# Hybrid trunk on one core: experts' tokens permuted once per layer, VectorE adds the result from PSUM

## What is computed

```python
g_prob = softmax(h @ wg + bg);  g_p, g_idx = top_k(g_prob, 1)
e_p, e_idx = top_k(softmax(e_logits of that group), 2)
gate = g_p * e_p / sum(e_p)
for e in range(16):
    a = silu(h @ w_gate[e]) * (h @ w_up[e])
    y = y + combine[:, e] * (a @ w_down[e])
return x + y
```

## Time and profile before

| | us |
|---|---|
| median of three runs | 1746.99 |
| the profiled execution | 1747.63 |
| its span, first to last instruction | 1745.8 |
| TensorE busy in the span | 1637.6 (94%) |
| VectorE busy | 1432.2 (82%) |
| ScalarE busy | 1087.4 (62%) |
| GpSimd busy | 91.3 (5%) |

### The profile page before, as it was taken

One profiled execution on the slowest core, in us unless ns is written; L12 is line 12 of the kernel. 1 busy time (PEld: TensorE's weight loads), 2 busy tenths in 40 slices (PEclk: granted clock), 3 DMA queues, 4 the chain that ended last, 5 costly groups with the idle time before them and its releaser, 6 DMA issues.

```text
span 1745.8 us, 22647 instructions
## 1 busy us (share of the span) xinstructions
PE 1637.6 (94%) x7933; PEld 1343.1 (77%) x7933; DVE 1432.2 (82%) x1625; ACT 1087.4 (62%) x1274; POOL 91.3 (5%) x71
## 2 busy tenths in 40 slices
PE   5999987987899999999999997799999999999998
PEld 4999873466688878878887885688877887887886
DVE  4476778865599899899989976679989989998996
ACT  4443433043477777677777764267777877777784
POOL 0000010000000020030011000000020003003000
PEclk9999998987899999999999998699999999999999
DMA  9654431442599789889979983269979988997991
GB/s 313 215 181 147 161 127 49 145 169 97 182 375 377 295 329 379 332 286 378 377 273 335 383 315 111 90 225 376 373 279 343 374 323 309 380 379 249 367 374 77
DMA packets 99917, 473.41 MB, mean 271 GB/s; under 512 B 18506, under 2 KB 21852, under 8 KB 49668
## 3 DMA queue, kind: packets, MB, share of 16 engines
q1 hardware_dynamic: 93508, 465.59, 72.4%
q10 hardware_dynamic: 6336, 6.88, 1.2%
HBM read 470.32 MB, written 2.11 MB: 271 GB/s over the span
## 4 chain that ended last, share of the span: by engine, by line
PE 76%; DVE 12%; issue 7%; ACT 3%; DMA 1%; ACTq 1%; POOL 0%; DVEq 0%; POOLq 0%
PE ps L1419 22%; PE ps L1421 21%; PE ps L1420 21%; DVE split_lo L937 6%; PE ps L1501 3%; PE ps L1681 3%; DVE cat L937 2%; DVE xn L933 2%; PE ps L1662 1%; PE ps L1385 1%; ACT split_hi L596 1%; PE ps L1530 1%; ACT xn L604 1%; ACT cat L596 1%; DVE work L1297 0%
## 5 line engine op out<-in xcount | busy, mean ns | idle before, releaser
L937 DVE TENSOR_TENSOR split_lo<-ring,split_hi 128x1024 fp32r<-128x1024 f32 x864 | 1082.5, 1273 | 163.0 <-ACT split_hi L596 117.4
L596 ACT ACTIVATE split_hi<-ring 128x1024 fp32r<-128x1024 f32 x864 | 909.6, 1059 | 329.4 <-PE ps L1421 310.8
L1419 PE MATMUL ps<-split_hi,cat 128*128 128x512 f32 (+1 forms) x1728 | 686.9, 398 | 23.0 <-DVE cat L937 14.1
L1421 PE MATMUL ps<-split_hi,cat 128*128 128x512 f32 (+1 forms) x1728 | 673.3, 390 | 0.0
L1420 PE MATMUL ps<-split_lo,cat 128*128 128x512 f32 (+1 forms) x1728 | 673.0, 389 | 0.0
L1419 PEld LDWEIGHTS ps<-split_hi,cat 128*128 128x128 f32 x1728 | 325.7, 188 | 117.8 <-DVE split_lo L937 31.6
L1421 PEld LDWEIGHTS ps<-split_hi,cat 128*128 128x128 f32 x1728 | 325.7, 188 | 68.2
L1420 PEld LDWEIGHTS ps<-split_lo,cat 128*128 128x128 f32 x1728 | 326.2, 189 | 63.6 <-issue 0.5
L584 POOL TENSOR_TENSOR x_sb<-work,x_sb 128x512 f32<-128x512 f32 x48 | 81.1, 1690 | 947.1 <-ACT work L596 947.1
L1419 PE MATMUL ps<-cat,split_hi 128*128 128x256 f32 x384 | 111.4, 290 | 5.1 <-DVE split_lo L937 5.1
L1420 PE MATMUL ps<-cat,split_hi 128*128 128x256 f32 x384 | 109.7, 286 | 0.0
(11 more groups left out here) (155 smaller groups left out, 693.4 us busy)
## 6 DMA issues: line engine op xcount, KB each, us to landing
ring<-in_w_gate SPq DMA_DIRECT2D x128, 1024.0 KB, 5.6
ring<-in_w_up SPq DMA_DIRECT2D x128, 1024.0 KB, 5.6
ring<-in_w_down SPq DMA_DIRECT2D x128, 1024.0 KB, 5.9
ring<-in_w_in_e SPq DMA_DIRECT2D x32, 1024.0 KB, 5.0
ring<-in_w_out_e SPq DMA_DIRECT2D x16, 1024.0 KB, 5.1
ring<-in_pool_w_o SPq DMA_DIRECT2D x4, 1024.0 KB, 8.3
x_sb<-in_x SPq DMA_DIRECT2D x2, 1024.0 KB, 7.1
ring<-in_w_in_e SPq DMA_DIRECT2D x8, 256.0 KB, 4.7
```

What stands on the lines that cost most here:

```text
L596: return nc.scalar.activation(out, in_, ACT.Copy, scale=scale)
L937: return tt(dst, full, hi.bitcast(F32), ALU.subtract)
L1419: mm(out, sh, mh, start=start, stop=False, **how)
L1421: return mm(out, sl, mh, start=False, stop=stop, **how)
```

## The change

The tokens of a layer are permuted once, behind the ranks, into group order: `pick` is 256 columns wide, and 32 matmuls of 128x256 fill `sorted_x`, which takes the place of `xn`. Each pass then takes 128 neighbouring places of it, from `window[p]` on: ScalarE and VectorE copy and split them from SBUF into `hgT`, at an offset read at run time. The ranks need 14 matmuls in place of 5. TensorE gathers nothing in a pass, `UNITS` has the last up projection ahead of the down projection of expert 2, and `turn_act(3)` stands inside that down projection. ScalarE's copies to `stage` and GpSimd's adds are gone; VectorE adds from PSUM in every pass.

```diff
-UNITS = [... (3, "g"), (2, "d"), (3, "u"), (3, "d")]
+UNITS = [... (3, "g"), (3, "u"), (2, "d"), (3, "d")]
-GATHER_BANK = (0, 1, 0, 1)
+GATHER_BANK = (0, 1, 4, 5, 6, 7, 4, 5)
...
-actT = cat_cut(2 * D, FC, P)
+actT = [cat_cut(2 * D + i * 2 * FF, FC, P) for i in range(2)]
...
# GpSimd
-def add_passes(l):
...
-                        nc.gpsimd.tensor_tensor(cols, stage[:, i % STAGES, :], cols, ALU.add).then_inc(m["x_moved"], 1)
...
# ScalarE
-                for q in range(4):
-                    slots_hi(0, q)
+                for i in range(8):
+                    act.wait_ge(m["gathered"], i + 1)
...
+                    copy(sorted_x[:, two, :], both).then_inc(m["sorted_out"], 1)
+                    copy(hgT[0][:, two, :], both[:, :, 0:P]).then_inc(m["slots_hi"], 1)
...
+                    w = act.value_load(window_i[0:1, bass.ds(p + (l * NPASS + 1), 1)], min_val=0, max_val=P)
...
-                            copy(stage[:, i % STAGES, :], ps[:, BANK_Y + i % 4, :]).then_inc(m["staged"], 1)
...
-                    split(p, gate + 12, 92)
-                    for q in range(3):
-                        slots_hi(p + 1, q)
+                    split(p, gate + 12, 84)
+                    slots_hi(p + 1, 0, w)
+                    split(p, 84, 88)
                     turned(EPG - 1)
...
# VectorE
+                    low(hgT[1][:, two, :], sorted_x[:, two, 0:P], hgT[0][:, two, :]).then_inc(m["gather_out"], 1)
...
+                    w = dve.value_load(window_i[0:1, bass.ds(p + (l * NPASS + 1), 1)], min_val=0, max_val=P)
...
                         split(p, 4 + i, 5 + i)
+                        if not first_pass and i in SCATTER_AT:
+                            add_y(p - 1, SCATTER_AT.index(i))
...
-                    for q in range(3):
-                        slots_lo(p + 1, q)
+                    split(p, 84, 86)
+                    slots_lo(p + 1, 0, w)
+                    split(p, 86, 89)
                     turned_lo(EPG - 1)
+                    split(p, 89, 91)
+                    slots_lo(p + 1, 1, w)
...
# TensorE
-                gather(0)
+                pe.wait_ge(m["pick_ready"], 1)
+                for i in range(8):
+                    if i >= 6:
+                        pe.wait_ge(m["slots_hi"], i - 3)
+                    for k in (2 * i, 2 * i + 1):
+                        for t in range(NT):
+                            last = mm(ps[:, GATHER_BANK[i], (k % 2) * SEQ:(k % 2 + 1) * SEQ],
+                                      sorted_x[:, k, t * P:(t + 1) * P], pick[:, t, :], start=t == 0, stop=t == NT - 1)
+                    last.then_inc(m["gathered"], 1)
...
+                            if fresh and (first_pass or q % 2 == 0):
+                                pe.wait_ge(m["gather_out"], q + 1 if first_pass else p * 4 + (q // 2 + 5))
...
-                                gather(p + 1, range(3))
-                                turn_act(e)
-                                gather(p + 1, range(3, 4))
+                        elif e == EPG - 2:
+                            down(e, lambda n: turn_act(EPG - 1) if n == 4 else None)
```

More of the change, by code:

```diff
@@ L243, in build @@
         act, o3 = cut(o3, 512)
-        pick, o3 = cut(o3, NT, P)
+        pick, o3 = cut(o3, NT, 2 * P)
         comb_now, o3 = cut(o3, NT, EPG)
@@ L262, in build @@
         cnt, o3 = cut(o3, NG)
+        lower, o3 = cut(o3, NT, NG)
+        late, o3 = cut(o3, NT, 1)
+        window, o3 = cut(o3, NPASS)
         assert o3 <= GAIN_AT
@@ L354, in build @@
                 "actT_done", "actT_out", "slots_hi",
[L355 removed]
+                "actT_hi", "sorted_out", "y_hi", "y_lo", "scattered", "x_moved", "hi", "lo", "used")})
             moe[l]["in"] = [sem(f"moe_in{l}_{s}") for s in range(RING)]
@@ L1210, in moe_dve @@
                 first_max(oneh, glog, col(0))
+                chain(tt(lower, prio.unsqueeze(1).to_broadcast([P, NT, NG]), gmax.to_broadcast([P, NT, NG]), ALU.is_lt))
                 tick_off().then_inc(m["rank_in"], 1)
@@ L1279, in add_y @@
                     tt(cols, ps[:, BANK_Y + b, :], cols, ALU.add).then_inc(m["x_moved"], 1)
-                for q in range(4):
-                    slots_lo(0, q)
+                for i in range(8):
+                    dve.wait_ge(m["slots_hi"], i + 1)
+                    two = slice(2 * i, 2 * i + 2)
+                    low(hgT[1][:, two, :], sorted_x[:, two, 0:P], hgT[0][:, two, :]).then_inc(m["gather_out"], 1)
                 def one_pass(p, first_pass=False):
+                    w = dve.value_load(window_i[0:1, bass.ds(p + (l * NPASS + 1), 1)], min_val=0, max_val=P)
                     def gate(e):
@@ L1311, in one_pass @@
                         split(p, 4 + i, 5 + i)
+                        if not first_pass and i in SCATTER_AT:
+                            add_y(p - 1, SCATTER_AT.index(i))
                         if i == 8:
                             gate(0)
-                    split(p, 16, 20)
+                    for u in range(16, 20):
+                        split(p, u, u + 1)
+                        if not first_pass and u - 4 in SCATTER_AT:
+                            add_y(p - 1, SCATTER_AT.index(u - 4))
                     times_up(0)
@@ L1686, in moe_pe @@
-                gather(0)
+                for t in range(NT):
+                    cols = slice(8 * t, 8 * t + NG)
+                    mm(ps[:, BANK_T, cols], before, oneh[:, t, :], start=True, stop=False)
+                    if t:
+                        mm(ps[:, BANK_T, cols], ones[:], oneh[:, 0, :], start=False, stop=False)
+                    mm(ps[:, BANK_T, cols], ones[:], lower[:, 0, :], start=False, stop=False)
+                    mm(ps[:, BANK_T, cols], ones[:], lower[:, 1, :], start=False, stop=True)
@@ new lines, in moe_pe @@
+                for at, what in ((16, oneh), (24, lower)):
+                    mm(ps[:, BANK_T, at:at + NG], ones[:], what[:, 0, :], start=True, stop=False)
+                    mm(ps[:, BANK_T, at:at + NG], ones[:], what[:, 1, :], start=False, stop=True)
+                mm(ps[:, BANK_T, 32:32 + NG], before, oneh[:, 0, :], start=True, stop=True)
+                mm(ps[:, BANK_T, 40:40 + NG], before, oneh[:, 1, :], start=True, stop=False)
+                mm(ps[:, BANK_T, 40:40 + NG], ones[:], oneh[:, 0, :], start=False, stop=True).then_inc(m["rank_done"], 1)
@@ L1774, in moe_pe @@
                 for i in range(8):
-                    scatter(more + (NG - 1), i, True)
+                    scatter(more + (NG - 1), i)
             moe_pe(0)
```

146 lines of the change are left out of this document (65 added, 81 removed).

## The result

The changed kernel takes 1683.8 us (median of four runs, 1682.82 to 1685.87), the kernel before, beside it on the same chip, 1747.0 (1745.36 to 1749.21): a ratio of 0.9639, interval 0.9622 to 0.9656, so 63.2 us less where 57.0 were forecast.

A forecast was written before the change was run, and what follows sets the result against it. TensorE's issue was taken to bound the kernel, with 4.0 us of waits a pass for VectorE's splits. Gathers -62.4, stall -18, offset +2 and starts +21.4 gave -57.0 us: from 1746.99 to 1690.0 us, range 1677 to 1716.

The forecast's parts named there:

- The likeliest case: Whole kernel: the prediction's own forecast of 1690.0 us, all of 1683 to 1698, given 0.65.
- The gathers in the passes: TensorE in eight passes: each loses 7.8 us of gather issue, -62.4 us, with no other engine's work showing beneath.
- The stall: TensorE's waits for VectorE's `split_lo` in six passes: 3 of 4.0 us go in each, -18 us.
- The weighing of the Trainium skill's rule: VectorE against GpSimd's adds: rule's whole-add exclusion (1688 ns each) set aside for about 1 us per add from the rows.
- The offset read at run time: Once a pass on each engine: 0.25 us taken for each of eight passes, +2 us.
- The start: Start of both layers: dearer ranks, wider gather and longer wait for unit 4 in layer 0, +21.4 us, bounds +14 and +27.
- VectorE did not become the bound at the turn of a pass: Rival, chance 0.12: VectorE's reserve fails at the turn of a pass, 24 us lost, 1714 us.
- The transfers did not either: Rival, chance 0.06: DMA transfers bind if only 355 GB/s hold over a whole pass, +26, 1716 us.
- ping-pong at `add_y`: Rival, chance 0.03: VectorE waits at its adds for TensorE's scatter, holding up the next splits; slower than before, 1756 us.
- What would show it: Signs in the changed profile: pass 138 to 139.5 us, splits 1.21 to 1.24 us, VectorE 0.94 busy, gather 16 to 17 us.

The follow-up runs named there:

- `old_order`: Changed kernel with the old order of units: the last expert's transposes between the last up and last down projection, gather still once per layer; 1747.3 us, ratio 1.0007.
- `adds_alone`: Kernel before with only VectorE adding y from PSUM, ScalarE's copies to `stage` and GpSimd's adds removed, gathers kept in the passes; 1728.2 us, ratio 0.9894.
- `pool_issues`: Changed kernel with layer 0's six transfers issued by GpSimd instead of ScalarE; 1673.8 us, ratio 0.9579.
- `half_bytes`: Changed kernel moving only half of each expert block, except the first eight of a layer; 1683.8 us, ratio 0.9641.
- `gather_alone`: Changed kernel with ScalarE's copies to `stage` and GpSimd's adds put back; 1703.9 us, ratio 0.9758.
- `idle_copies`: Changed kernel plus, behind each of 48 scatters, an idle GpSimd copy of one 128x512 tile after a one-column add that waits; 1685.0 us, ratio 0.9654.

## Why the prediction was right, step by step

The likeliest case came in: forecast 1690.0, measured 1683.8, in the range 1677 to 1716 and at the lower edge of 1683 to 1698. By stretches of the two profiled executions:

| stretch | predicted | measured |
|---|---|---|
| six passes of the loop | 6 x -10.55 = -63.3 | 6 x -11.0 = -66.0 |
| two first passes (from unit 4 on) | 2 x -7.55 = -15.1 | -8.2 - 8.0 = -16.2 |
| the starts of the layers' experts, to unit 4 | +21.4 | +10.4 + 8.1 = +18.5 |
| the rest of the program | 0 | -0.9 |
| together | -57.0 | -64.6 |

- *The gathers in the passes, -7.8 each.* Right: by the distances between TensorE's starts a pass held 7.82 us of gather and now holds none. But the sentence that no other work lies under it that would now show holds only with the new order. `old_order` shows 4.9 us of waits there (5.5 with what lies around them), and the clock's fall behind them, 2.4. The prediction moved the transposes and costed the move at nothing, which was right; it did not say that this move carries the rest.
- *The stall, -3 a pass.* Nearly: products 134.69 to 132.33, scatter 4.54 to 3.82, transposes 1.72 to 1.63, together -3.2. The mechanism was shown, with its own size: 18.8 us in `adds_alone` against 18 forecast.
- *The weighing of the Trainium skill's rule.* The price was right and the reading wrong. I took the 1688 ns of GpSimd's record for the length of the exclusion, and so saw 1 us per addition as less than that rule says. The record holds GpSimd's own wait for the running split; what is left is 1.15 us, and the trace agrees with the rule in full.
- *The offset read at run time, +2.* Mis-sized, it is nothing that can be seen: unit 0 starts 15.60 us behind the gather's start with both of TensorE's reads in between, and 8 x 0.427 + 56 x 0.216 of gather alone make 15.5.
- *The start, +21.4.* The largest miss, 3 us. The ranks cost +3.7 each where 4.1 were forecast (+3.9 and +0.2); the gather 15.6 us and not 16.5, since only its first eight instructions ran at half clock where I had taken eleven, and the reads cost nothing: +8.1 and +8.0 to unit 0 against 10.1. In layer 0 the wait for unit 4 grew from 5.98 to 8.22 us, 1 us more than I had allowed, and `pool_issues` shows that all of it is ScalarE's issuing: without it unit 4 stands 5.68 us behind unit 0, as in layer 1 (5.67).
- *The rivals.* VectorE did not become the bound at the turn of a pass: it is busy for 0.955 of the pass, and TensorE waits for no `split_lo`; some 1.0 us of waits for `y_lo` is left. The transfers did not either (`half_bytes`). No ping-pong at `add_y`.
- *What would show it.* A pass of 138 to 139.5 us (138.15), no gather in it, splits at 1.21 to 1.24 us (1216 ns), VectorE at 0.94 or more (0.955), about 363 GB/s (364): all came. The gather, said to take 16 to 17 us, took 15.6.

Two differences are no more than spread. Layer 0's router starts 1.8 us sooner (418.05 us against 419.88), ahead of all that the change touches; over the profiles of all fourteen kernels it starts between 417.99 and 421.53. And `gather_alone` costs 20.1 us where excess less additions makes 18.4, which lies within the intervals.

## What to carry to other kernels

An engine's work that is taken away was perhaps cover for another engine's step: look at what waited under it, and move that step in the same change, or the time comes back as a wait, and here with a slower clock behind it. When two engines exclude each other, read the one's duration only from the other's end on, and price it by the sum of the slowed instructions' excess. Where the slowed engine has no reserve, as beside the scatters here, that sum is the change in time: it agreed three times within the noise (29.5 for 29.3, 16.5 for 16.9, 18.4 for 18.8). An experiment that finds no cost should be read in its timeline first: in `idle_copies` six of 48 copies met what they were meant to disturb.

## What the runs showed of the hardware

A GpSimd addition or copy that reads SBUF and a VectorE split with two SBUF inputs shut each other out: the later one waits for the other's end, in both directions (an addition ends 1.13 to 1.17 us behind a split's end, a split 1.07 to 1.18 us behind GpSimd's). Even a one-column addition of 0.19 us took up to 1.17 us. A VectorE operation with one input in PSUM kept its 0.68 us beside them, and a split its 1.23 us beside a fill. Issuing one and the same transfer took ScalarE 5.66 us and GpSimd 0.56, by their records. TensorE's idle stretches of 3.40 and 1.49 us, with four transposes between them, were followed by products 0.43 us apart at half clock until 747.9; idle products in the same gaps kept the clock at 1.00.
